# The second down projection reads its split weights and activations 64 bytes further in their partitions

## The chip, the cores and the metric
One core of one Trainium2 chip. The metric is the device time of the whole program in microseconds (us), as the median of several runs.

## What is computed
Two decoder blocks in float32, one after the other, on 512 tokens of width 1024, each with a mixing part and a feed-forward part (FFN). What matters here is the second block's FFN, whose last product is the second down projection:

```python
FFN_HIDDEN = 2816
h = rms_norm_2(x, norm_ffn_g[l])
up = causal_dwconv(h @ w_up[l], conv_ffn_w[l])
a, b = jnp.split(up, 2, axis=-1)
x = x + (jax.nn.silu(a) * b) @ w_down[l]     # [512, 2816] @ [2816, 1024]
...
return rms_norm_2(x, norm_f_g)
```

## The kernel before
**Split products.** TensorE multiplies in fp32r, so each float32 operand is kept as a high part (ScalarE's copy to fp32r) and a low part (VectorE's difference of the float32 value and the high part). Each product is three matmuls into the same place of PSUM: high by high, high by low, low by high. In most stages the weights are the stationary operand (loaded into the array, 128 columns) and the activations move (256 or 512 columns): `product` at L2516, L2519 and L2522, and lines L2783 to L2785 and L2857 to L2859. In the value projections of both blocks (`slab_v`) and in the second down projection it is the other way round: the activations are stationary and 512 columns of weights move. The profile names a matmul's operands as psum<-moving,stationary.

**Weights.** They come from memory in slabs of up to 2048 float32 values a partition, into `raw`, `x_buf`, `y_buf` and other homes. ScalarE writes a slab's high part into `w_hi` in two halves (L989, L990) and VectorE its low part into `w_lo` (L1541, L1544). `w_hi` and `w_lo` are rings of two slabs, 4096 values a partition; `W_AT[s]` is where slab s starts, and `w_at` (L660) gives the view that both the writers and TensorE use. TensorE waits for `w_lo_half` or `w_lo_ready` before a slab, and ScalarE waits for TensorE to be done with the slab that was there before.

**The second down projection.** It is computed as seven products of half the rows, half the hidden width and half the columns (`PRODUCTS`), some on sums of quarters, each in three parts (`SUBS`: 4, 4 and 3 chunks of 128 hidden values). So there are 21 weight slabs and 21 activation parts. A part of 1024 or 768 values a partition is split by ScalarE into `part_hi` (`split_part`, L1136) and by VectorE into `part_lo` (L1785), both of 11 chunks of 256 tokens. For each chunk k and each 128 tokens m of its half, `rows_product` makes three matmuls with the 128 token columns stationary and 512 weight columns moving: 21 parts, 77 chunks, 154 calls. Its lines are L3065 (high, high), L3066 (high, low) and L3067 (low, high). After parts 1 and 4 TensorE also transposes x (`turn_x`, L3054). The first down projection uses the same `part_hi` and `part_lo` as moving operands of 256 columns (L2857 to L2859). After the last product the rows are summed, normalised and stored.

**The order of the work** is written out by hand for each engine, with semaphores between them; nothing is planned at run time.

**Where operands start.** Every tensor has a fixed byte offset within a partition, from the sizes of those allocated ahead of it. Within these tensors every operand of a split product starts at a multiple of 512 bytes. Offsets before:

| tensor | byte offset | past a multiple of 128 |
|---|---|---|
| w_hi | 49280 | 0 |
| w_lo | 65664 | 0 |
| act_hi, act_lo | 104640, 121024 | 64 |
| m_hi | 137408 | 64 |
| part_hi and s_hi0 (s_at) | 182464 | 64 |
| part_lo | 193728 | 64 |
| x_buf0 | 204992 | 64 |

The moving and stationary operands of the split products outside these (s_lo, s2_hi, s2_lo, m_lo, z_hi, z_lo) also start 64 bytes past a multiple of 128.

Of the kernel before, what the change touches and what calls it, by code (L numbers as in the profile page):

```python
# [14 lines left out]
F32 = mybir.dt.float32  # L15
F32R = mybir.dt.float32r
BF16 = mybir.dt.bfloat16
ALU = mybir.AluOpType
ACT = mybir.ActivationFunctionType

P = 128
# [13 lines left out]
SLAB = 2048  # L35
COLS_A = SLAB // DC
ROWS_B = SLAB // WIDTH
FFN_STEPS = FF // COLS_A
CAUSAL = sum(TOKENS - P * b for b in range(TB))
HALF = TOKENS // 2  # L40
KH = FC // 2
# [27 lines left out]
def _add(w, kind, k0, nk, c0, nc_, home=None):  # L69
    SLABS.append((w, kind, k0, nk, c0, nc_))  # L70
    HOME.append(home or ("raw", sum(h[0] == "raw" for h in HOME), 0))
    return len(SLABS) - 1


def _cols_a(w, c0, n):
    first = len(SLABS)
    for j in range(n // COLS_A):
        _add(w, "A", 0, DC, c0 + j * COLS_A, COLS_A)
    return first
# [15 lines left out]
def _seven(w):  # L95
    first = len(SLABS)
    for place, stage, (kh, nh), _ in PRODUCTS:
        for j, (k0, nk) in enumerate(SUBS):
            _add(w, "B", kh * KH + k0, nk, nh * WIDTH, WIDTH, (place, j, stage) if place != "raw" else None)
    return first  # L100
# [5 lines left out]
S_K = _cols_a("w_in", 3 * WIDTH, WIDTH)  # L106
S_V = _add("w_in", "B", 0, ROWS_B, 4 * WIDTH, WIDTH)
_add("w_in", "B", ROWS_B, ROWS_B, 4 * WIDTH, WIDTH)
S_OUT_LRU = _add("w_out", "B", 0, WC, 0, WIDTH)
_add("w_out", "B", 0, WC, WIDTH, WIDTH)  # L110
S_OUT_ATT = _add("w_out", "B", WC, WC, 0, WIDTH)
_add("w_out", "B", WC, WC, WIDTH, WIDTH)
FIRST_SEVEN, LAST = 2, FFN_STEPS - 1

# [36 lines left out]
S_DOWN = _seven("w_ffn_out")  # L151
# [35 lines left out]

S_V2 = _add("w_in_2", "B", 0, ROWS_B, 5 * WIDTH, WIDTH)
_add("w_in_2", "B", ROWS_B, ROWS_B, 5 * WIDTH, WIDTH)
S_OA2 = _add("w_out_attn_2", "B", 0, WC, 0, WIDTH)  # L190
# [40 lines left out]
S_DOWN2 = _seven("w_down_2")  # L231
# [3 lines left out]
W_AT, W_PREV = [], []  # L235
# [76 lines left out]
def bank_of(g):  # L312

    if g == GROUP[S_F2]:
        return OUT_BANKS[0]
    if g == GROUP[S_Q2B]:
        return bank_of(GROUP[S_K2 + 1])
    return 2 if g == GROUP[S_Q2] else 4 * (g % 2)
# [56 lines left out]
def two_blocks(nc, t, out):  # L375
    with ExitStack() as ctx:
        def sb(name, shape, dt=F32, where=None):
            return (where or ctx).enter_context(nc.sbuf_tensor(name, shape, dt))

        def sem(name):  # L380
            return ctx.enter_context(nc.semaphore(name))
# [2 lines left out]
        x_base = (nc.sbuf_base + 31) // 32 * 32  # L384
        xT = sb("xT", [P, DC, TOKENS])
        raw = sb("raw", [P, 2, SLAB])
        w_hi = sb("w_hi", [P, 2, SLAB], F32R)
        w_lo = sb("w_lo", [P, 2, SLAB], F32R)
        scratch_base = (nc.sbuf_base + 31) // 32 * 32
        tmp = sb("tmp", [P, 6, TOKENS])  # L390
        rstd = sb("rstd", [P, 3, TOKENS])
# [19 lines left out]
        scope = ExitStack()  # L411
        hid = sb("hid", [P, FC, TOKENS], F32, scope)
        part_hi = sb("part_hi", [P, KH * HALF], F32R, scope)
        part_lo = sb("part_lo", [P, KH * HALF], F32R, scope)
        x_buf = [sb("x_buf0", [P, SLAB], F32, scope), sb("x_buf1", [P, SLAB], F32, scope),
                 sb("x_buf2", [P, 3 * WIDTH], F32, scope)]
        hid_at = act_base + 8 * DC * TOKENS
        s_at = hid_at + 4 * FC * TOKENS
        xg = nc.alloc_sbuf_tensor_at("xg", [P, DC, TOKENS], F32, offset=hid_at + 4 * 12 * TOKENS)
        s_hi = [nc.alloc_sbuf_tensor_at(f"s_hi{k}", [P, WC * HALF], F32R, offset=s_at + d) for k, d in enumerate((0, 8192, 28672, 36864))]  # L420
        s_lo = [nc.alloc_sbuf_tensor_at(f"s_lo{k}", [P, WC * HALF], F32R, offset=s_at + 4096 + d) for k, d in enumerate((0, 8192, 28672, 36864))]
# [132 lines left out]
        sum_made, part_hi_ready, part_lo_ready = sem("sum_made"), sem("part_hi_ready"), sem("part_lo_ready")  # L554
# [84 lines left out]
        def quarter(n):  # L639

            kh, th = PRODUCTS[n // 3][3]
            k0, nk = SUBS[n % 3]
            return hid[:, kh * KH + k0:kh * KH + k0 + nk, th * HALF:(th + 1) * HALF]
# [5 lines left out]
        def part_view(x, n):  # L649

            k0, nk = SUBS[n % 3]
            return x[:, k0 * HALF:(k0 + nk) * HALF].rearrange("p (k n) -> p k n", k=nk)
# [6 lines left out]

        def w_at(x, s, a, n):  # L660

            return x.rearrange("p a n -> p (a n)")[:, W_AT[s] + a:W_AT[s] + a + n]

        gates, gate_conv, rest_2, kept_1 = scratch[:, 2:4], scratch[:, 4:6], scratch[:, 0], scratch[:, 8]

# [308 lines left out]
        def _(act):  # L974
            A = nc.scalar.activation
# [151 lines left out]
            def split_part(n, s_down=S_DOWN):  # L1127

                if n >= N_PARTS:
                    return  # L1130
                if n >= 3:
                    act.wait_ge(slab_done, s_down + n - 2)
                made = {1: 0, 3: 3, 4: 6, 5: 9}.get(n // 3)
                if made is not None:
                    act.wait_ge(sum_made, made + n % 3 + 1 + (12 if s_down == S_DOWN2 else 0))
                A(part_view(part_hi, n), quarter(n), ACT.Copy).then_inc(part_hi_ready, 1)  # L1136

            def keep_product(bank, dst):

# [26 lines left out]
            for e in range(S_FFN + 1, S_DOWN):  # L1166
# [23 lines left out]
                if (kind, i) == ("p5", LAST - 1):  # L1190
                    act.wait_ge(slab_done, e + 1)
                    for n in range(3):
                        split_part(n)
            act.wait_ge(ffn_hidden, 2 * FFN_STEPS)
            for n in range(N_PARTS - 1):
# [222 lines left out]
            for e in range(S_UP + 2 * SECOND_SEVEN + 1, S_DOWN2):  # L1418
# [34 lines left out]
                if (kind, i) == ("p5", LAST - 1):  # L1453
                    act.wait_ge(slab_done, e + 1)
                    act.wait_ge(up_hidden, 12)
                    for n in range(3):
                        split_part(n, S_DOWN2)
# [23 lines left out]
            for n in range(N_PARTS - 1):  # L1481
                split_w(S_DOWN2 + n + 2)
                split_part(n + 3, S_DOWN2)
                if n in (2, 5):
                    act.wait_ge(up_hidden, 2 * LAST)
                    act.wait_ge(ffn_hidden, 2 * FFN_STEPS + 2)
                    act.wait_ge(slab_done, S_DOWN2 + n + 1)
# [23 lines left out]
        def _(dve):  # L1511
            V = nc.vector
# [267 lines left out]
            def split_part(n, second=0):  # L1780

                if n >= N_PARTS:
                    return
                dve.wait_ge(part_hi_ready, n + 1 + N_PARTS * second)
                V.tensor_tensor(part_view(part_lo, n), quarter(n), part_view(part_hi, n).bitcast(F32),  # L1785
                                ALU.subtract).then_inc(part_lo_ready, 1)

            def gate_out(i, b):
# [51 lines left out]
            def first_sum_lo(k):  # L1840

                dve.wait_ge(sums_hi_ready, k + 1)
                V.tensor_tensor(s_lo[k].rearrange("p (k n) -> p k n", k=WC), xg_block(*SUM_PLACE[k]),
                                s_hi[k].rearrange("p (k n) -> p k n", k=WC).bitcast(F32), ALU.subtract).then_inc(sums_lo_ready, 1)

            for e in range(S_FFN, S_DOWN):
# [49 lines left out]
                if (kind, i) == ("p4", FIRST_SEVEN):  # L1896
                    first_sum_lo(1)
            dve.wait_ge(ffn_hidden, 2 * FFN_STEPS)

# [507 lines left out]
            dve.wait_ge(up_hidden, 2 * LAST)  # L2407
            dve.wait_ge(ffn_hidden, 2 * FFN_STEPS + 2)

# [81 lines left out]
        def _(pe):  # L2491
# [22 lines left out]
            def product(dst, stationary, moving, first, last, after_one=None, after_two=None):  # L2514

                ins = mm(dst, stationary[0], moving[0], start=first, stop=False)  # L2516
                if after_one:
                    after_one(ins)
                ins = mm(dst, stationary[0], moving[1], start=False, stop=False)  # L2519
                if after_two:  # L2520
                    after_two(ins)
                return mm(dst, stationary[1], moving[0], start=False, stop=last)  # L2522

            def w_part(s, k, c0, n):

                at = k * SLABS[s][5] + c0
                return w_at(w_hi, s, at, n), w_at(w_lo, s, at, n)

            def act_part(chunk, t0=0, n=TOKENS):
                return act_hi[:, chunk, t0:t0 + n], act_lo[:, chunk, t0:t0 + n]  # L2530
# [28 lines left out]
            def slab_v(s, part, before=lambda k: None, first=range(TB), ahead=lambda tb: None):  # L2559
# [4 lines left out]
                b = bank_of(GROUP[s])  # L2564
                for k in range(ROWS_B):
                    before(k)
                    for tb in first if k == 0 else range(TB):
                        if k == 0:
                            ahead(tb)
                        ins = product(psum[:, b + tb], act_part(ROWS_B * part + k, tb * P, P), w_part(s, k, 0, WIDTH),  # L2570
                                      part == 0 and k == 0, part == 1 and k == ROWS_B - 1)
# [33 lines left out]
            for s in range(S_V):  # L2605
# [7 lines left out]
                if s == 0:  # L2613
# [3 lines left out]
                    n = NROWS - FIRST_ROWS  # L2617
# [244 lines left out]
            pe.wait_ge(z_m0, LAST - FIRST_SEVEN)  # L2862
            pe.wait_ge(ffn_hidden, 2 * FFN_STEPS - 2)
            for n in range(N_PARTS):
# [193 lines left out]
            def rows_product(n, k, m):  # L3058

                dst = psum[:, PRODUCT_BANK[n // 3] + m]  # L3060
                fresh = n % 3 == 0 and n // 3 not in (2, 4) and k == 0
                at = (SUBS[n % 3][0] + k) * HALF + m * P
                hi, lo = part_hi[:, at:at + P], part_lo[:, at:at + P]
                wh, wl = w_part(S_DOWN2 + n, k, 0, WIDTH)
                mm(dst, hi, wh, start=fresh, stop=False, skip_group_check=True)  # L3065
                mm(dst, hi, wl, start=False, stop=False, skip_group_check=True)  # L3066
                return mm(dst, lo, wh, start=False, stop=True, skip_group_check=True)  # L3067
# [79 lines left out]
```

## Time and profile before

| | us |
|---|---|
| median of 3 runs | 1256.82 |
| lowest and highest run | 1256.01, 1268.97 |
| span of the profiled execution, first to last instruction | 1253.8 |

The profile records one execution; it gives its span, and no other time of its own. The span leaves out what lies before the first and after the last instruction, so it stands beside the runs, not among them. A matmul's record is longer than the distance to the next one's start, since they are pipelined: the pace is read from starts. Offsets of tensors are not in the profile; they are in the table above.

### The profile page before, as it was taken

Reading aid. Unit: us, or ns where it says so; the run is one execution under the profiler, and the core shown is the slowest. Engines: PE = TensorE matmul, PEld = TensorE weight load, DVE = VectorE, ACT = ScalarE, POOL = GpSimd, SP = SyncE. Lnnn points to the kernel's source line nnn. Section 1 sums busy time; section 2 is a strip of 40 time slices with the busy share of each in tenths; the row PEclk is TensorE's granted clock in tenths of the full one; section 3 lists DMA queues with packets and bytes.
Section 4 is the critical chain, followed back from the end, with each engine's and each line's share of the span. In section 5 each row is a group of like instructions: output and inputs, shape, how many; then the busy total and the mean of one; then the engine's idle time right before and its main releaser. Section 6 shows DMA issues by size and latency. Waiting matters only on the chain.

```text
span 1253.8 us, 19172 instructions
## 1 busy us (share of the span) xinstructions
PE 1228.0 (98%) x7804; PEld 1078.1 (86%) x7804; DVE 991.8 (79%) x1196; ACT 670.4 (53%) x837; POOL 186.0 (15%) x168
## 2 busy tenths in 40 slices
PE   6999999999999999999999999999999999999997
PEld 5778677889999999997899999657888999988886
DVE  6888764888788778887989967566678899989886
ACT  5463674374545445567545535363444666656555
POOL 5003001002222101110122113000000222202020
PEclk9999999999999999999999999999999999999999
DMA  5423201249999779664599857301324799968765
GB/s 172 143 68 98 70 1 34 84 123 194 177 208 184 142 204 248 141 123 118 111 210 197 190 101 206 113 1 34 117 86 151 125 213 194 183 157 173 207 116 137
DMA packets 144458, 174.14 MB, mean 139 GB/s; under 512 B 5370, under 2 KB 118250, under 8 KB 144242
## 3 DMA queue, kind: packets, MB, share of 16 engines
q0 software_dynamic: 58288, 71.33, 35.7%
q1 hardware_dynamic: 86066, 101.58, 24.3%
q8 instruction: 62, 1.02, 0.3%
q14 instruction: 26, 0.21, 0.1%
q10 hardware_dynamic: 16, 0.00, 0.0%
HBM read 170.78 MB, written 2.11 MB: 138 GB/s over the span
## 4 chain that ended last, share of the span: by engine, by line
PE 92%; DVE 4%; ACT 2%; issue 1%; DMA 0%; SPq 0%; ACTq 0%; DVEq 0%
PE psum L2516 12%; PE psum L2522 12%; PE psum L2519 12%; PE psum L2785 11%; PE psum L2783 11%; PE psum L2784 11%; PE psum L2857 3%; PE psum L2859 3%; PE psum L2858 3%; PE psum L3065 2%; PE psum L3066 2%; PE psum L3067 2%; PE psum L2974 1%; PE psum L2660 1%; PE psum L2645 1%; PE psum L2672 1%
## 5 line engine op out<-in xcount | busy, mean ns | idle before, releaser
L990 ACT ACTIVATE w_hi<-raw 128x1024 fp32r<-128x1024 f32 (+2 forms) x121 | 156.2, 1294 | 210.5 <-PE psum L2522 145.6
L1544 DVE TENSOR_TENSOR w_lo<-raw,w_hi 128x1024 fp32r<-128x1024 f32 (+2 forms) x121 | 184.4, 1526 | 57.2 <-ACT w_hi L990 57.2
L2516 PE MATMUL psum<-act_hi,w_hi 128*128 128x512 f32 x520 | 207.7, 399 | 4.3 <-DVE act_lo L1551 1.5
L2522 PE MATMUL psum<-act_hi,w_lo 128*128 128x512 f32 x520 | 204.7, 394 | 0.1
L2519 PE MATMUL psum<-act_lo,w_hi 128*128 128x512 f32 x520 | 203.6, 391 | 0.0
L2785 PE MATMUL psum<-s_hi,w_lo 128*128 128x256 f32 x704 | 194.9, 277 | 0.0
L2783 PE MATMUL psum<-s_hi,w_hi 128*128 128x256 f32 x704 | 194.8, 277 | 0.0
L2784 PE MATMUL psum<-s_lo,w_hi 128*128 128x256 f32 x704 | 194.8, 277 | 0.0
L2785 PE MATMUL psum<-act_hi,w_lo 128*128 128x256 f32 x528 | 146.2, 277 | 0.0
L2783 PE MATMUL psum<-act_hi,w_hi 128*128 128x256 f32 x528 | 146.1, 277 | 0.0
L2784 PE MATMUL psum<-act_lo,w_hi 128*128 128x256 f32 x528 | 146.1, 277 | 0.0
L2784 PEld LDWEIGHTS psum<-s_lo,w_hi 128*128 128x128 f32 x704 | 132.2, 188 | 0.2
L2783 PEld LDWEIGHTS psum<-s_hi,w_hi 128*128 128x128 f32 x704 | 132.0, 188 | 0.2
L2785 PEld LDWEIGHTS psum<-s_hi,w_lo 128*128 128x128 f32 x704 | 132.2, 188 | 0.0
L2516 PEld LDWEIGHTS psum<-act_hi,w_hi 128*128 128x128 f32 x520 | 97.6, 188 | 31.0 <-issue 6.4
L2519 PEld LDWEIGHTS psum<-act_lo,w_hi 128*128 128x128 f32 x520 | 97.7, 188 | 22.6 <-issue 1.7
L2522 PEld LDWEIGHTS psum<-act_hi,w_lo 128*128 128x128 f32 x520 | 97.7, 188 | 20.8
L2784 PEld LDWEIGHTS psum<-act_lo,w_hi 128*128 128x128 f32 x528 | 99.1, 188 | 0.3
L2783 PEld LDWEIGHTS psum<-act_hi,w_hi 128*128 128x128 f32 x528 | 99.0, 188 | 0.3
L2785 PEld LDWEIGHTS psum<-act_hi,w_lo 128*128 128x128 f32 x528 | 99.1, 188 | 0.0
L1544 DVE TENSOR_TENSOR w_lo<-xz,w_hi 128x1024 fp32r<-128x1024 f32 x60 | 73.2, 1220 | 21.8 <-ACT w_hi L990 20.1
L2857 PE MATMUL psum<-part_hi,w_hi 128*128 128x256 f32 x308 | 85.0, 276 | 0.0
(411 smaller groups left out, 2672.6 us busy)
## 6 DMA issues: line engine op xcount, KB each, us to landing
raw<-in_w_in SPq DMA_DIRECT2D x15, 1024.0 KB, 5.4
xz<-in_w_ffn_in POOLq DMA_DIRECT2D x24, 512.0 KB, 6.6
raw<-in_w_ffn_in SPq DMA_DIRECT2D x22, 512.0 KB, 5.5
xz<-in_w_up POOLq DMA_DIRECT2D x21, 512.0 KB, 6.1
raw<-in_w_up SPq DMA_DIRECT2D x18, 512.0 KB, 5.2
raw<-in_w_in SPq DMA_DIRECT2D x16, 512.0 KB, 5.0
v<-in_w_in POOLq DMA_DIRECT2D x15, 512.0 KB, 6.2
x_buf<-in_w_ffn_out POOLq DMA_DIRECT2D x6, 1024.0 KB, 9.8
```

The lines of the kernel that those rows point to most:

```text
L990: A(w_at(w_hi, s, h, n - h), home(s, n)[:, h:n], ACT.Copy).then_inc(w_hi_ready, 1)
L1544: V.tensor_tensor(w_at(w_lo, s, h, n - h), home(s, n)[:, h:n], w_at(w_hi, s, h, n - h).bitcast(F32), ALU.subtract).then_inc(w_lo_ready, 1)
L2516: ins = mm(dst, stationary[0], moving[0], start=first, stop=False)
L2519: ins = mm(dst, stationary[0], moving[1], start=False, stop=False)
L2522: return mm(dst, stationary[1], moving[0], start=False, stop=last)
L2783: mm(dst, wh, hi, start=kind not in ("p2", "p4") and k == 0 and m == 0, stop=False, skip_group_check=True)
L2784: mm(dst, wh, lo, start=False, stop=False, skip_group_check=True)
L2785: ins = mm(dst, wl, hi, start=False, stop=True, skip_group_check=True)
L2857: mm(dst, wh, hi, start=fresh, stop=False, skip_group_check=True)
L2858: mm(dst, wh, lo, start=False, stop=False, skip_group_check=True)
L2859: return mm(dst, wl, hi, start=False, stop=True, skip_group_check=True)
L3065: mm(dst, hi, wh, start=fresh, stop=False, skip_group_check=True)
```

## The change
The second down projection uses operands that lie 64 bytes further. The two weight buffers become flat and 32 values longer, so that slabs from `S_DOWN2` on can start 16 values (64 bytes) later in them; the activation parts of the second down projection get views `row_hi` and `row_lo` that start 64 bytes past `part_hi` and `part_lo`; a pad of 32 values stands behind `part_lo`. ScalarE and VectorE write, and TensorE reads, through the moved views. With the longer buffers, `w_lo` starts 128 bytes later, all tensors behind it 256 bytes later, and `x_buf` 384. In the second down projection the moving operands then start at 49344 (w_hi) and 65856 (w_lo), 64 bytes past a multiple of 128, and the stationary ones at 182784 and 194048, on a multiple. Everything else keeps its offset within 128 bytes.

```diff
+MOVED = 16
...
-        w_hi = sb("w_hi", [P, 2, SLAB], F32R)
-        w_lo = sb("w_lo", [P, 2, SLAB], F32R)
+        w_hi = sb("w_hi", [P, 2 * SLAB + 2 * MOVED], F32R)
+        w_lo = sb("w_lo", [P, 2 * SLAB + 2 * MOVED], F32R)
...
         part_lo = sb("part_lo", [P, KH * HALF], F32R, scope)
+        sb("part_rest", [P, 2 * MOVED], F32, scope)
...
+        row_hi = nc.alloc_sbuf_tensor_at("row_hi", [P, KH * HALF], F32R, offset=s_at + 4 * MOVED)
+        row_lo = nc.alloc_sbuf_tensor_at("row_lo", [P, KH * HALF], F32R, offset=s_at + 4 * KH * HALF + 4 * MOVED)
...
         def w_at(x, s, a, n):
 
-            return x.rearrange("p a n -> p (a n)")[:, W_AT[s] + a:W_AT[s] + a + n]
+            at = W_AT[s] + (MOVED if s >= S_DOWN2 else 0)
+            return x[:, at + a:at + a + n]
...
-                A(part_view(part_hi, n), quarter(n), ACT.Copy).then_inc(part_hi_ready, 1)
+                A(part_view(part_hi if s_down == S_DOWN else row_hi, n), quarter(n), ACT.Copy).then_inc(part_hi_ready, 1)
...
-                V.tensor_tensor(part_view(part_lo, n), quarter(n), part_view(part_hi, n).bitcast(F32),
+                hi, lo = (row_hi, row_lo) if second else (part_hi, part_lo)
+                V.tensor_tensor(part_view(lo, n), quarter(n), part_view(hi, n).bitcast(F32),
                                 ALU.subtract).then_inc(part_lo_ready, 1)
...
-                hi, lo = part_hi[:, at:at + P], part_lo[:, at:at + P]
+                hi, lo = row_hi[:, at:at + P], row_lo[:, at:at + P]
```

## Rows read from the trace of the kernel before
**Rows 1.** the page of the kernel before: head, busy table, granted clock
```profile
span 1253.8 us, 19172 instructions
...
PE 1228.0 (98%) x7804; PEld 1078.1 (86%) x7804; DVE 991.8 (79%) x1196; ACT 670.4 (53%) x837; POOL 186.0 (15%) x168
...
PEclk9999999999999999999999999999999999999999
```
**Rows 2.** the page: the chain that ended last, by engine
```profile
PE 92%; DVE 4%; ACT 2%; issue 1%; DMA 0%; SPq 0%; ACTq 0%; DVEq 0%
```
**Rows 3.** one line's instructions: L3065 between 1165.5 and 1246 us
```profile
L3065 PE MATMUL psum<-w_hi,part_hi x116: 393/398/479, 1165.3 to 1245.8; 128*128 128x512 f32 x116
```
**Rows 4.** the same view: L2516 between 922.4 and 976.5 us
```profile
L2516 PE MATMUL psum<-act_hi,w_hi x79: 388/388/397, 922.7 to 976.2; 128*128 128x512 f32 x79
```
**Rows 5.** stretches: window, length, TensorE busy (instructions seen), granted clock, DMA share, GB/s
```profile
632.00:672.00 40.00, 40.00 (x342) 1.00 1.03 208
934.00:974.00 40.00, 40.00 (x177) 1.00 0.37 120
1000.00:1040.00 40.00, 40.00 (x355) 1.00 0.99 192
```
**Rows 6.** timeline of TensorE at 778 us; start us, us, engine, line, out<-moving,stationary
```profile
778.43 0.40 PE L2516 MATMUL psum<-w_hi,act_hi 128*128 128x512 f32 x1
...
779.13 0.39 PE L2516 MATMUL psum<-w_hi,act_hi 128*128 128x512 f32 x1
...
779.83 0.40 PE L2516 MATMUL psum<-w_hi,act_hi 128*128 128x512 f32 x1
```
**Rows 7.** timeline of TensorE across the start of the second down projection
```profile
1134.69 0.28 PE L2784 MATMUL psum<-act_lo,w_hi 128*128 128x256 f32 x1
1134.80 0.28 PE L2785 MATMUL psum<-act_hi,w_lo 128*128 128x256 f32 x1
1134.92 0.39 PE L3065 MATMUL psum<-w_hi,part_hi 128*128 128x512 f32 x1
...
1135.61 0.39 PE L3065 MATMUL psum<-w_hi,part_hi 128*128 128x512 f32 x1
...
1137.01 0.39 PE L3065 MATMUL psum<-w_hi,part_hi 128*128 128x512 f32 x1
```
**Rows 8.** timeline of TensorE across 618 us
```profile
616.96 0.39 PE L2516 MATMUL psum<-act_hi,w_hi 128*128 128x512 f32 x1
...
618.33 0.28 PE L2783 MATMUL psum<-act_hi,w_hi 128*128 128x256 f32 x1
...
619.04 0.28 PE L2783 MATMUL psum<-act_hi,w_hi 128*128 128x256 f32 x1
```
**Rows 9.** one line's instructions: L2516 between 54.5 and 64.8 us
```profile
L2516 PE MATMUL psum<-act_hi,w_hi x15: 397/397/398, 54.7 to 64.5; 128*128 128x512 f32 x15
```
**Rows 10.** waits between 1130 and 1254 us: total us, times, longest
```profile
ACT w_hi L989 <- PE psum L3067: 31.4, 16, 3.1
...
PEld psum L3065 <- DVE w_lo L1541: 0.5, 1, 0.5
```
**Rows 11.** stretch 1182 to 1222 us: PE, PEld, DVE, ACT, POOL busy, clock, DMA
```profile
1182.00:1222.00 40.00, 40.00 (x173) 32.25 (x172) 36.80 (x35) 22.90 (x29) 7.80 (x6) 1.00 0.51 89
```
**Rows 12.** groups of ScalarE by shape, 1134 to 1254 us
```profile
L1136 ACT ACTIVATE part_hi<-hid 128x1024 fp32r<-128x1024 f32 x12 | 12.6, 1047 | 5.9 <-DVE hid L1911 5.9
L989 ACT ACTIVATE w_hi<-x_buf 128x1024 fp32r<-128x1024 f32 x7 | 7.4, 1056 | 6.4 <-PE psum L3067 6.0 <-PE psum L2785 0.5
```
**Rows 13.** groups of TensorE by shape, whole span
```profile
L2516 PE MATMUL psum<-act_hi,w_hi 128*128 128x512 f32 x520 | 207.7, 399 | 4.3 <-DVE act_lo L1551 1.5 <-DVE act_lo L1553 1.5 <-DVE w_lo L1544 0.6
...
L2783 PE MATMUL psum<-s_hi,w_hi 128*128 128x256 f32 x704 | 194.8, 277 | 0.0
...
L2783 PE MATMUL psum<-act_hi,w_hi 128*128 128x256 f32 x528 | 146.1, 277 | 0.0
...
L2857 PE MATMUL psum<-part_hi,w_hi 128*128 128x256 f32 x308 | 85.0, 276 | 0.0
```

## The prediction
> **What bounds the kernel now.** I read the head of the page first. TensorE is busy 98% of a span of 1253.8 us, and its granted clock is 9 tenths or more in every slice, so the clock stays at the higher of its two levels (2.4 GHz) and takes no part in what follows [rows 1]. Then the chain that ended last: 92% of it is TensorE, so the time is the number of matmuls times the distance between their starts, and little else [rows 2]. A busy share of 98% says nothing of that distance, because a matmul's record overlaps the next one's. So I took starts.
>
> In the second down projection 116 starts of L3065 lie between 1165.3 and 1245.8 us. Each is followed by one of L3066 and one of L3067, so 115 x 3 = 345 steps take 80.5 us: 233.3 ns a step [rows 3]. In the first slabs of the second FFN, also 512 columns wide, 79 starts of L2516 lie between 922.7 and 976.2 us: 78 x 3 = 234 steps in 53.5 us, 228.6 ns a step [rows 4]. Both stretches run without a stop and at the same clock. The stage that the change touches is thus paced about 4.7 ns a matmul slower than its neighbour.
>
> Two more places tell what goes with the slow pace. The value projection of the second block is built as the down projection is, with split weights moving and split activations stationary; six steps from 778.43 to 779.83 us are 1.40 us, again 233.3 ns [rows 6]. And the pace changes at the border, with no stop between: up to 1134.80 us the steps of 256 columns are 0.11 us, and from 1135.61 to 1137.01 us six steps of the down projection take 1.40 us [rows 7]. What the two slow stages share is where their operands start. By the offsets in the section on the kernel, moving w_hi and w_lo start on a multiple of 128 bytes and stationary activations 64 bytes past one. In every other split product of the kernel it is the other way round.
>
> The slow pace is not bound to those offsets alone. At 618.33 us the steps go from 228 ns (616.96 to 618.33 us is 1.37 us for six) at 512 columns to 118 ns (0.71 us for six) at 256 [rows 8], and they stay there: of 40 us the stretch at 632 us holds 342 matmuls and the one at 1000 us 355 [rows 5]. 40/342 less 40/355 is 4.3 ns, the same surplus per matmul, though those activations move from 64 bytes past a multiple of 128. So do those of 54.7 to 64.5 us, where 42 steps take 9.8 us, 233.3 ns [rows 9]. I read this as two paces between which TensorE's stream falls: moving operands on a multiple of 128 always got the long one (the value projections and all of the down projection), the others nearly always the short one.
>
> **The change, part by part.** It adds no instruction, no wait and no DMA.
>
> *Buffers.* w_hi and w_lo grow by 128 bytes a partition each, and a pad of 128 bytes stands ahead of the x buffers. So w_lo starts 128 bytes later, everything allocated behind it 256, and x_buf 384. All of these are multiples of 128, so no product outside the second down projection changes its offset within 128 bytes. DMA, ScalarE and VectorE do the same work at addresses of the same kind: cost 0.
>
> *Moved writers.* For the 21 weight slabs ScalarE and VectorE write 64 bytes further, and for the 21 activation parts too. Rows of both kinds of address exist: copies of 128x1024 to part_hi (64 past) take 1047 ns, and to w_hi (on the multiple) 1056 ns [rows 12]. They swap, so the sum over the stage is bounded by 9 ns each way for each of some 60 copies, 0.5 us of ScalarE's time. None of it is on the path: ScalarE waits 31.4 us in this stage for TensorE to give buffers back, against 0.5 us that TensorE waits for VectorE's w_lo [rows 10]. I take 0.
>
> *Moved operands of TensorE.* 154 x 3 = 462 matmuls. Afterwards the moving weights start 64 bytes past a multiple of 128 and the stationary activations on one, which is the arrangement of rows 4. If the pace goes with it, each step shrinks by 4.7 ns by rows 3 and 4, or 4.3 ns by the pair in rows 5: 462 x 4.7 = 2.2 us or 462 x 4.3 = 2.0 us. I take 2.1 us. The bounds are 0 (the pace doesn't care) and, below nothing, nothing that a row shows for this stage: it already has the longest pace that any split product of its width has.
>
> The Trainium skill has a rule that would make the gain larger. In "TensorE: Matmul & The Clock Gate", section "Back-to-back issue gap", a warm matmul of N columns costs N/2.4 + 2.5 ns, which is 215.8 ns for 512. An estimate by that page is (233.3 - 215.8) x 462 = 8.1 us. No long stretch of this trace goes below 228.6 ns [rows 4], so the measurement decides and the sum stays at 2.1 us.
>
> *The feeders.* If TensorE wants its slabs 2% sooner, ScalarE and VectorE must give them sooner. Between 1182 and 1222 us TensorE is busy all 40 us, VectorE 36.8, ScalarE 22.9 [rows 11]. The 173 matmuls seen there would need about 0.8 us less; VectorE has 3.2 us to spare. Its cover thins but holds, and were it gone, the stage would keep at most its old pace. Nothing new is late after the last matmul: mean square, root, scaling and store follow as before.
>
> *Sum.* 1253.8 - 2.1 = 1251.7 us of span. The profile gives no time of its own beside the span; the median of the runs shown, 1256.82 us, lies 3.0 us above it. With the same 3.0 us the forecast is 1254.7 us, 0.17% faster, where about 1% is what a measurement of this kernel tells from no change.
>
> **The rivals.**
>
> *The offset does nothing: 1256.8 us.* The down projection is slow for another reason, say that its weights come through the moving side, or that its stream starts in the long pace after the two rounds of transposes at L3054 and stays there. For it: the long pace also occurs with the good offsets [rows 8, 9], so offset and pace are not one thing. Against it: form and operand sizes are those of rows 4, and the switch at the border of the stage comes with no pause [rows 7].
> The Trainium skill speaks for this rival too: "SBUF — State Buffer", section "Who interferes with whom", gives TensorE two independent read ports, one for the moving operand and one for the weight load, that never wait for anyone, and its note on cachelines makes 16 bytes the unit; by both a shift of 64 bytes changes nothing. That the trace has two paces at one clock doesn't fit these rules by itself.
>
> *The change also frees the stretch of 618 to 714 us: 1251.2 us.* All buffers behind w_hi move, so that stream may fall into the short pace. Some 96 us / 0.1177 us = 816 steps by 4.3 ns are 3.5 us more, 1254.7 - 3.5. For it: nothing in offsets within 128 bytes holds that stretch in the long pace, so something finer does. Against it: the same something may be the timing of its first step, which isn't touched.
>
> *A long stretch outside falls into the long pace: slower.* The distance from w_hi to w_lo goes from 16384 to 16512 bytes in every stage, and the split products load from both in turn. If that distance, or the address within 256 bytes (of which w_lo's changes), selects the pace, stretches that are short now become long. Outside the touched stage there are at least (520 + 704 + 528 + 308) x 3 = 6180 such matmuls [rows 13], less the 816 and 48 that are long already: about 5300 at 4.3 ns is 22.8 us, and the time is 1254.7 + 22.8 = 1277.5 us, 1.6% slower. It decides from about 490 matmuls on (2.1 us / 4.3 ns), where the gain is eaten, and from 3400 on it is over 1%. For it: rows 8 show that one border suffices to turn over 800 matmuls. Against it: of the long streams with moving operands 64 past, only two short or middling ones turned.
>
> **How the numbers follow.** Offset selects the pace: 0.68, 1254.7 us. No effect: 0.19, 1256.8 us. Also the stretch at 618 us: 0.07, 1251.2 us. A stretch outside turns long: 0.06. The range runs from 1250.5 us (the third case, less the 0.8 us by which the two nearest runs of the kernel before differ) to 1260.0 us: no effect, 0.8 us of spread, and a stretch of some 550 matmuls turned long (2.4 us). The whole of the last rival is left out. Faster by over 1% needs 12.6 us, which no case gives: 0.02. Slower by over 1% needs more than half of all matmuls outside to turn, or something unseen: 0.04. Within 1%: 0.94.
>
> **What would show it.** Right: the line view of L3065 has a step of about 229 ns instead of 233.3 in its last 80 us, the durations of its records fall from a median of 398 ns towards 390, a window of 40 us there holds some 176 matmuls instead of 173, and from the first matmul of the stage to its last it is about 2 us shorter. The value projection at 778 us stays at 233.3 ns. The copies to w_hi in that stage take about 1050 ns. Wrong: the step of L3065 stays at 233.3 ns (second case); the counts of 40 us at 632 or 1000 us change (the other two); or TensorE waits more than 1 us for w_lo in this stage, which would mean that VectorE's cover is gone.

## The result, and the profile after

| | us |
|---|---|
| changed kernel, median of 6 runs (lowest, highest) | 1272.07 (1271.17, 1273.75) |
| kernel before, median of 6 runs (lowest, highest) | 1256.45 (1254.03, 1268.97) |
| ratio, with its 95% interval | 1.0111 (1.0083 to 1.0139) |
| span of the profiled execution, before and after | 1253.8, 1271.1 |

The kernel got 1.1% slower, where 0.2% faster was forecast. The page of the changed kernel, as far as it answers to [rows 1, 2]: head, busy table, granted clock and the chain that ended last, by engine.

```profile
span 1271.1 us, 19172 instructions
...
PE 1245.7 (98%) x7804; PEld 1093.2 (86%) x7804; DVE 994.7 (78%) x1196; ACT 671.5 (53%) x837; POOL 186.3 (15%) x168
...
PEclk9999999999999999999999999999999999999999
...
PE 95%; ACT 2%; DVE 2%; DMA 0%; issue 0%; SPq 0%; ACTq 0%
```

The same number of instructions, the same clock, and 17.7 us more of TensorE. The chain is TensorE still. So the steps got longer, and the first thing to see is where. One line's instructions (durations, first and last start): L2863 is the first matmul of the *first* down projection, which has 256 columns and no operand moved. First the kernel before, then the changed one.

```profile
L2857 PE MATMUL psum<-part_hi,w_hi x308: 276/276/276, 460.6 to 564.9; 128*128 128x256 f32 x154
```

```profile
L2863 PE MATMUL psum<-part_hi,w_hi x308: 278/279/280, 469.8 to 579.3; 128*128 128x256 f32 x154
```

From the first to the last of these 308 starts, 307 x 3 = 921 steps take 104.3 us before and 109.5 after: 113.2 and 118.9 ns a step. So a stage that the diff only displaces pays 5.2 us, more than the whole forecast. TensorE over stretches of 40 us, first the kernel before and then the changed one; the number in brackets counts matmuls:

```profile
320.00:360.00 40.00, 40.00 (x355) 1.00 0.97 198
665.00:705.00 40.00, 40.00 (x342) 1.00 0.96 181
```

```profile
320.00:360.00 40.00, 40.00 (x339) 1.00 0.93 184
665.00:705.00 40.00, 40.00 (x339) 1.00 1.00 192
1010.00:1050.00 40.00, 40.00 (x356) 1.00 1.02 200
```

At 320 us 355 matmuls became 339. At 665 us the kernel before was already slow (342), and it got a little slower (339). Of these three stretches only the one at 1010 us runs as before [rows 5]. In the second down projection itself, first the kernel before, then the changed one:

```profile
L3065 PE MATMUL psum<-w_hi,part_hi x154: 393/396/504, 1134.9 to 1245.8; 128*128 128x512 f32 x154
```

```profile
L3071 PE MATMUL psum<-w_hi,row_hi x154: 388/394/483, 1153.4 to 1263.1; 128*128 128x512 f32 x154
```

The stage takes 110.9 us from its first to its last start before, and 109.7 after: 1.2 us less, where 2.1 were forecast. The border of the stage, in the timeline (start, duration), answers to [rows 7]:

```profile
1153.25 0.28 PE L2791 MATMUL psum<-act_hi,w_lo 128*128 128x256 f32 x1
1153.37 0.39 PE L3071 MATMUL psum<-w_hi,row_hi 128*128 128x512 f32 x1
...
1154.06 0.40 PE L3071 MATMUL psum<-w_hi,row_hi 128*128 128x512 f32 x1
...
1155.45 0.39 PE L3071 MATMUL psum<-w_hi,row_hi 128*128 128x512 f32 x1
```

Six steps from 1154.06 to 1155.45 us take 1.39 us, 231.7 ns against 233.3 before. Over the whole stage the mean of triples of steps is 231.2 ns. The feeders answer to [rows 10], and nothing is wrong with them:

```profile
ACT w_hi L994 <- PE psum L3073: 30.8, 16, 3.0
...
PEld psum L3071 <- DVE w_lo L1546: 0.2, 1, 0.2
```

**Where the 17.3 us of span come from.** All steps of split products from the two traces' starts, taken three by three, with pauses left out:

| products | matmuls | ns a step before | after | us |
|---|---|---|---|---|
| 256 columns, activations move | 4620 | 114.12 | 117.57 | +15.9 |
| 512 columns, activations move | 1848 | 229.24 | 231.41 | +4.0 |
| value projections, weights move | 192 | 233.33 | 231.32 | -0.4 |
| second down projection, weights move | 462 | 233.32 | 231.19 | -1.0 |

The sum is 18.5 us. The 1.2 us by which the spans differ less lie in stops and at the borders of streams, which this count leaves out. The line to note is the third. The value projections got 2 ns a step shorter as well, though none of their operands was moved by 64 bytes.

### The profile page after: what moved, and what is told of

The parts are those of the page before. It is cut to its first block, busy times and chain, and to the rows that moved or that the text cites. A ratio compares the mean times of both kernels' runs of the same rounds, so it can differ in the third digit from the quotient of the medians.

```text
span 1271.1 us, 19172 instructions
## 1 busy us (share of the span) xinstructions
PE 1245.7 (98%) x7804; PEld 1093.2 (86%) x7804; DVE 994.7 (78%) x1196; ACT 671.5 (53%) x837; POOL 186.3 (15%) x168
## 3 DMA queue, kind: packets, MB, share of 16 engines
q8 instruction: 62, 1.02, 0.3%
## 4 chain that ended last, share of the span: by engine, by line
PE 95%; ACT 2%; DVE 2%; DMA 0%; issue 0%; SPq 0%; ACTq 0%
PE psum L2522 12%; PE psum L2528 12%; PE psum L2525 12%; PE psum L2790 12%; PE psum L2789 11%; PE psum L2791 11%; PE psum L2864 3%; PE psum L2863 3%; PE psum L2865 3%; PE psum L3073 3%; PE psum L3071 3%; PE psum L3072 3%; PE psum L2980 1%; PE psum L2666 1%; PE psum L2651 1%; PE psum L2678 1%
## 5 line engine op out<-in xcount | busy, mean ns | idle before, releaser
L2522 PE MATMUL psum<-act_hi,w_hi 128*128 128x512 f32 x520 | 210.5, 405 | 4.3 <-DVE act_lo L1558 1.7
L2790 PE MATMUL psum<-s_lo,w_hi 128*128 128x256 f32 x704 | 197.8, 281 | 0.0
L2864 PE MATMUL psum<-part_lo,w_hi 128*128 128x256 f32 x308 | 87.2, 283 | 0.0
```

The source lines that it names most:

```text
L2790: mm(dst, wh, lo, start=False, stop=False, skip_group_check=True)
L2864: mm(dst, wh, lo, start=False, stop=False, skip_group_check=True)
```

## The experiments

All time differences of under 0.5% or so drown in the spread of the kernel before (31 runs of one comparison lie between 1254.7 and 1270.1 us), so the step is the reading that decides and the time its check. "Distance" below is the byte offset of the moving operand less that of the stationary one, within 256. Before it is 64 for w_hi and w_lo alike where activations move, and 192 where weights move. In the changed kernel w_lo lies 128 bytes later and the activations 256, so the distance of w_lo is 192 in the first case and 64 in the second, while that of w_hi stays.

### Is it the 64 bytes, or the longer buffers?

**grow_only.** The buffers of the changed kernel, without the moves.
```diff
-            at = W_AT[s] + (MOVED if s >= S_DOWN2 else 0)
+            at = W_AT[s]
...
-offset=s_at + 4 * MOVED)
+offset=s_at)
...
-offset=s_at + 4 * KH * HALF + 4 * MOVED)
+offset=s_at + 4 * KH * HALF)
```


> The changed kernel with its buffers as long as there (w_lo 128 bytes later, all behind it 256), but with no operand moved by 64 bytes: the second down projection reads where the buffers begin. Theory A, the pace of a split product follows the distance between its moving and its stationary operand (bytes, within 256), so that w_lo's 128 bytes cost the time and the 64 bytes, which both operands share, do nothing: about 1272 us, as the changed kernel, and steps of 231.1 ns in the second down projection, as there. Theory B, the 64 bytes cost or give something: the time leaves 1272 us by more than 3 us, or the step of L3065 goes back to 233.3 ns. Theory C, all of it is luck of how streams start: anything between 1254 and 1272 us.

Measured: 1272.7 us, ratio to before 1.0101 (1.0073 to 1.0129). The stage of the second down projection and two stretches of 40 us:

```profile
L3071 PE MATMUL psum<-w_hi,row_hi x154: 387/394/478, 1152.8 to 1262.5; 128*128 128x512 f32 x154
```

```profile
320.00:360.00 40.00, 40.00 (x339) 1.00 0.94 184
1010.00:1050.00 40.00, 40.00 (x355) 1.00 1.02 200
```

109.7 us for the stage and 339 matmuls at 320 us: the readings of the changed kernel, without its 64 bytes. Both its loss and its small gain come from the longer buffers.

**wide256.** The changed kernel, moves and all, with w_hi and w_lo longer by 256 bytes instead of 128.
```diff
-        w_hi = sb("w_hi", [P, 2 * SLAB + 2 * MOVED], F32R)
-        w_lo = sb("w_lo", [P, 2 * SLAB + 2 * MOVED], F32R)
+        w_hi = sb("w_hi", [P, 2 * SLAB + 4 * MOVED], F32R)
+        w_lo = sb("w_lo", [P, 2 * SLAB + 4 * MOVED], F32R)
```


> The changed kernel with w_hi and w_lo longer by 256 bytes instead of 128, the 64-byte moves kept. w_lo then lies 256 bytes later than before and everything behind it 512. Theory A (distance within 256 bytes): every distance is that of the kernel before, so about 1256 us, with the second down projection at 233.3 ns a step in spite of its moved operands. Theory B (the 64 bytes matter): the second down projection isn't at 233.3 ns. If the distance counts within 512 bytes or more, the time stays near 1272 us.

Measured: 1256.68 us, ratio 0.9978 (0.9944 to 1.0013).

```profile
L3071 PE MATMUL psum<-w_hi,row_hi x154: 389/397/499, 1134.9 to 1245.8; 128*128 128x512 f32 x154
```

```profile
320.00:360.00 40.00, 40.00 (x356) 1.00 0.96 196
1010.00:1050.00 40.00, 40.00 (x355) 1.00 0.99 193
```

The loss is gone (356 matmuls at 320 us), and so is the gain: 110.9 us for the stage, 233.3 ns a step, with the moving operands 64 bytes past a multiple of 128 and the stationary ones on it. That is the arrangement on which the forecast rested, and it does nothing.

**all64.** The kernel before with 64 unused bytes ahead of w_hi.
```diff
+        sb("pad", [P, 16])
         w_hi = sb("w_hi", [P, 2, SLAB], F32R)
```


> The kernel before with 64 unused bytes ahead of w_hi, so that all tensors from w_hi on lie 64 bytes later and every distance between them stays. Theory A (distances): no change, 1254 to 1258 us, 233.3 ns in the down projection. The theory of the prediction (where the moving operand starts within 128 bytes): weights move 64 past a multiple of 128 and get 229 ns, and all other moving operands start on a multiple and get the long step, 5300 matmuls by 4.3 ns, about 1277 us.

Measured: 1260.89 us (1257.38 to 1271.33), ratio 1.0011 (0.9975 to 1.0047). 111.0 us for the stage, 355 matmuls at 320 us.

```profile
L3066 PE MATMUL psum<-w_hi,part_hi x154: 389/395/496, 1140.0 to 1251.0; 128*128 128x512 f32 x154
```

```profile
320.00:360.00 40.00, 40.00 (x355) 1.00 0.97 196
1010.00:1050.00 40.00, 40.00 (x346) 1.00 1.00 197
```

Every operand of the split products changed its offset within 128 bytes. The steps stayed: 229.3 ns where 512 columns of activations move, 233.3 where weights do, and at 256 columns the two paces that the kernel before has too (113.3 and 117.8 ns). By the forecast's reading this kernel was to take 1277 us. The stretch at 1010 us holds both of them (346 matmuls); more of that below.

**lo_only128.** The kernel before with w_lo and the scratch behind it 128 bytes later, and everything from act_hi on in its place.
```diff
         w_hi = sb("w_hi", [P, 2, SLAB], F32R)
+        decay = sb("decay", [P, WC])
+        f_bias = sb("f_bias", [HEADS, 1])
+        eps = sb("eps", [P, 2])
+        gain_both = sb("gain_both", [P, DC])
         w_lo = sb("w_lo", [P, 2, SLAB], F32R)
...
-        decay = sb("decay", [P, WC])
-        f_bias = sb("f_bias", [HEADS, 1])
-        eps = sb("eps", [P, 2])
-        gain_both = sb("gain_both", [P, DC])
```


> The kernel before with w_lo and the scratch tensors behind it 128 bytes later and nothing else: four small tensors of 128 bytes together go from behind the scratch to between w_hi and w_lo, so act_hi, part_hi and all later tensors stay. Theory A (distance of moving and stationary operand within 256 bytes): the distances are those of the changed kernel, 64 from w_hi and 192 from w_lo where activations move, so about 1272 us and 118.9 ns in most 256-column streams. If it was the shift of the activations by 256 bytes instead: 1254 to 1270 us, as before.

Measured: 1280.38 us, ratio 1.0172 (1.0121 to 1.0223).

```profile
L3065 PE MATMUL psum<-w_hi,part_hi x154: 388/394/478, 1161.8 to 1271.5; 128*128 128x512 f32 x154
```

```profile
320.00:360.00 40.00, 40.00 (x339) 1.00 0.94 184
1010.00:1050.00 40.00, 40.00 (x339) 1.00 0.96 191
```

The stage takes 109.7 us and the stretch at 320 us has 339 matmuls, as in the changed kernel, so the place of w_lo is enough (of the scratch that moved with it nothing is an operand of a split product). The time is 8 us above the expected. At 1010 us there are 339 matmuls here and 356 in the changed kernel: that stream of 1104 matmuls runs at 118.9 ns instead of 113.3, 6.1 us, and the products of 512 columns at 232.6 ns instead of 231.4, another 2.2 us.

### Does the distance set the pace?

**rows128.** The kernel before, only the activations of the second down projection 128 bytes further.
```diff
+        sb("part_rest", [P, 32], F32, scope)
...
+        row_hi = nc.alloc_sbuf_tensor_at("row_hi", [P, KH * HALF], F32R, offset=s_at + 4 * 32)
+        row_lo = nc.alloc_sbuf_tensor_at("row_lo", [P, KH * HALF], F32R, offset=s_at + 4 * KH * HALF + 4 * 32)
```
(and the uses of the two views as in the change.)

> The kernel before, and only the split activations of the second down projection 128 bytes further (w_hi and w_lo as before, a pad of 128 bytes ahead of x_buf). Moving less stationary address goes from 192 to 64 within 256 bytes, what the products with moving activations had before. Theory A: the step of L3065 falls from 233.3 to about 229 ns, 462 x 4.3 ns = 2.0 us less, the rest as before: about 1254 us. The theory of the prediction (offsets within 128 bytes): 233.3 ns, no change.

Measured: 1258.14 us, ratio 0.9967 (0.9929 to 1.0004), which is no difference that can be told.

```profile
L3069 PE MATMUL psum<-w_hi,row_hi x154: 388/394/501, 1137.1 to 1246.6; 128*128 128x512 f32 x154
```

109.5 us for the stage with 228.9 ns a step, where the kernel before has 110.9 and 233.3. The offsets within 128 bytes are those of before, so only the distance is new (x_buf moved too, but no product reads it). This is the gain that the forecast looked for; 462 x 4.4 = 2.0 us of it should show, and 1.4 do. In this execution TensorE's weight loads waited 0.8 us for w_lo in the stage and stood still another 0.4 us for no reason that the profile shows, against 0.5 us in all before.

**rows192** is the same with 192 bytes (`4 * 48`), so that the distance is 0.

> The kernel before, and only the split activations of the second down projection 192 bytes further, so that its moving and stationary operands are 0 apart within 256 bytes, the distance at which act192 had the shortest step for 512 columns (226.8 ns in this stage). Theory A: 226.8 ns a step against 233.3 ns, 462 x 6.5 = 3.0 us less than the kernel before in that stage, the streams elsewhere as before and with their luck: a median of 1252 to 1258 us. If the gain in act192 came from the whole kernel being shifted: 233.3 ns.

Measured: 1256.75 us, ratio 0.9995 (0.9965 to 1.0024).

```profile
L3069 PE MATMUL psum<-w_hi,row_hi x154: 387/389/504, 1135.4 to 1244.2; 128*128 128x512 f32 x154
```

```profile
PEld psum L3069 <- DVE w_lo L1544: 0.9, 1, 0.9
PEld psum L3069 <- issue: 0.5, 1, 0.5
```

The stage takes 108.8 us, 2.1 us less than before, at 226.8 ns a step. Two stops that the kernel before has only in part (0.9 and 0.5 us) eat the rest of the 3.0 us. The whole kernel can't be told from the one before: a stage's 2 us are below what the runs resolve.

**act32, act64, act128, act192, act224**: the kernel before with so many unused bytes behind w_lo, here for 64.
```diff
         w_lo = sb("w_lo", [P, 2, SLAB], F32R)
+        sb("pad", [P, 16])
```


> The kernel before with 64 unused bytes behind w_lo: weights stay, everything behind them lies 64 bytes later, so the distance of moving and stationary operand within 256 bytes goes from 64 to 128 where activations move, and from 192 to 128 where weights move. Theory A (distance sets the pace): both kinds of product get the same pace, one that the kernel before doesn't show; if pace grows with the distance it lies between 229 and 233.3 ns at 512 columns. If only offsets of one operand mattered, weights that move would stay at 233.3 ns.

> The kernel before with 128 unused bytes behind w_lo. Activations that move are then 192 from the weights, which is what the down projection had before, and weights that move are 64 from the activations. Theory A: the paces change sides: about 229 ns in the second down projection and the value projections (2.9 us less), 233.3 ns and about 118 ns always where activations move (some 5500 matmuls by 4.3 ns or more, 24 us and up): about 1277 to 1284 us. Theory of the prediction (offset within 128 bytes): nothing changes, 1254 to 1260 us.

> The kernel before with 192 unused bytes behind w_lo: all distances are 0 within 256 bytes. Theory A: one pace for both kinds of product. By a reading in which the two streams of reads meet in the same place it is the longest of all; by one in which they then run in step it is the shortest. Either way far from the time before if pace and distance are tied: below 1250 or above 1262 us.

> The kernel before with 32 unused bytes behind w_lo: distance 96 where activations move, 160 where weights move. Theory A with a pace that grows smoothly with the distance: between before (64) and act64 (128) for moving activations. If only whole steps of 64 bytes count, it equals one of the two.

> The kernel before with 224 unused bytes behind w_lo: distance 32 where activations move, 224 where weights move. Fills the gap between 0 (act192) and 64 (before). Theory A: paces between these two, so 227 to 229 ns at 512 columns; at 256 columns 113.3 to 120 ns. If steps of 64 bytes count alone, it equals act192 or the kernel before. Any value that all 256-column streams keep below 117 ns would be a place without luck.

Measured, as ratios to before: act32 1289.06 us, 1.0245 (1.02 to 1.0291); act64 1283.74 us, 1.0205 (1.0167 to 1.0242); act128 1270.25 us (1259.55 to 1272.22), 1.0071 (1.0038 to 1.0103); act192 1275.7 us, 1.0141 (1.0104 to 1.0178); act224 1274.25 us, 1.0126 (1.0082 to 1.0169). For act128, the stage and the two stretches of 40 us; then the stage and the same stretches for act192:

```profile
L3066 PE MATMUL psum<-w_hi,part_hi x154: 388/394/505, 1150.0 to 1259.2; 128*128 128x512 f32 x154
```

```profile
320.00:360.00 40.00, 40.00 (x342) 1.00 0.94 186
1010.00:1050.00 40.00, 40.00 (x355) 1.00 1.03 205
```

```profile
L3066 PE MATMUL psum<-w_hi,part_hi x154: 389/389/499, 1157.7 to 1266.1; 128*128 128x512 f32 x154
```

```profile
320.00:360.00 40.00, 40.00 (x336) 1.00 0.91 182
1010.00:1050.00 40.00, 40.00 (x335) 1.00 1.00 196
```

With act128 the sides are changed: the stage runs at 228.9 ns, and all 512-column products with moving activations at 233.3. With act192 the stage is the shortest of all (108.4 us), while 256 columns are at their slowest (336). Stretches of act32, of act64 and of act224:

```profile
320.00:360.00 40.00, 40.00 (x336) 1.00 0.91 182
1010.00:1050.00 40.00, 40.00 (x335) 1.00 0.96 183
```

```profile
320.00:360.00 40.00, 40.00 (x336) 1.00 0.92 182
1010.00:1050.00 40.00, 40.00 (x339) 1.00 0.97 188
```

```profile
320.00:360.00 40.00, 40.00 (x345) 1.00 0.96 188
1010.00:1050.00 40.00, 40.00 (x345) 1.00 1.02 199
```

All kernels together: the steady paces, from the starts in their traces, in ns a step (activations moving, or weights moving where marked *). The mean of a stage or of a kind of product lies up to 0.6 ns above them, since it holds borders and short stretches of another pace.

| distance | 512 columns | 256 columns |
|---|---|---|
| 0 (act192; rows192*) | 226.7; 226.7* | 120.0 |
| 32 (act224) | 233.3 | 116.7 or 117.8 |
| 64 (before; rows128*) | 228.9, one stretch 233.3; 228.9* | 113.3 or 117.8 |
| 96 (act32) | 233.3 | 120.0 |
| 128 (act64) | 232.6; 232.5* | 118.7 or 120.0 |
| 160 (act32) | 234.2* | |
| 192 (act128; before*) | 233.3; 233.3* | 113.3 or 117.8 |
| 224 (act224) | 233.3* | |
| w_hi 64, w_lo 192 (changed kernel) | 228.9 or 233.3 | 118.9, one stream 113.3 |
| w_hi 192, w_lo 64 (changed kernel) | 231.2* | |

At each distance where both kinds were seen (0, 64, 128 and 192, all at 512 columns), it doesn't matter which of the operands moves. The distance decides which paces occur, with no simple order: for 512 columns 0 is best and 64 next; for 256 columns 0 is worst and only 64 and 192 reach 113.3. In the last two rows w_hi and w_lo lie at different distances, and there the distance of each matmul by itself doesn't give the pace: 118.9 ns is longer than both paces seen at 64 alone and at 192 alone (113.3 and 117.8). Whether the change from one distance to the other counts, or the distance between w_hi and w_lo, no run separates.

My expectations of act128 (256 columns always long), act32 (between its neighbours) and act224 (512 columns near 228 ns) were wrong, because the paces don't follow the distance in order.

### Two paces at one distance

Three more profiles of unchanged kernels, the kernel before twice and the changed one once.

> The kernel before, unchanged, profiled once more. If the pace of a 256-column stream is drawn anew in each execution, the streams at 289, 458, 618, 750 and 980 us (113.3 but for 618 us, which had 117.8) come out otherwise here, and the span with them: 4.45 ns for each of their 1248, 948, 816, 240 and 1104 matmuls that turns. If addresses and program alone decide, they come out as in the first profile and the span is 1253.8 us within 1 us.

> The kernel before, unchanged, a third profile: as for the second. The runs of this kernel so far lie between 1254 and 1270 us; with 4.45 ns a matmul the streams that turn should account for the difference of this span from 1253.8 us within 1 us.

> The changed kernel, unchanged, profiled once more. Theory A with two paces: the first four 256-column streams at 118.9 ns again, and a time of 1270 to 1274 us; the fifth, of 1104 matmuls, which had 113.3 ns in its first profile, may come out at 118.9 ns and the span 6.1 us longer. If the fifth is short by its place in the program, it is at 113.3 ns again.

Measured: 1255.98 us (span 1254.2), 1257.5 us (span 1255.7), and 1275.01 us (span 1273.3) for the changed one. TensorE in the stream at 618 us, first before_again, then before_third:

```profile
640.00:655.00 15.00, 15.00 (x134) 1.00 1.14 215
665.00:705.00 40.00, 40.00 (x355) 1.00 0.96 182
```

```profile
640.00:655.00 15.00, 15.00 (x135) 1.00 1.08 213
665.00:705.00 40.00, 40.00 (x342) 1.00 0.96 182
```

In the first profile of this same program the stretch from 665 us held 342 matmuls. Here it holds 355 and 342, and at 640 us the third profile still has the short pace (135 in 15 us). Between them, at 658 us, TensorE stopped for 1.6 us, and the stream came back in the long one. So the pace isn't set by program and addresses alone, nor by the chip: before_again and before_third ran on the same one. A stream takes one of its paces where it starts, and keeps it for hundreds of matmuls until something breaks its rhythm. A stop can turn it or leave it (before_again stopped for 0.3 us at 659 us and came back at 113.3 ns), and it takes no stop: in all64 a single step of 134 ns at 1022 us, 20 ns longer than the others, is where the stream goes from 113.3 to 117.8 ns for good:

```profile
1022.11 0.28 PE L2786 MATMUL psum<-s_hi,w_lo 128*128 128x256 f32 x1
1022.23 0.30 PE L2784 MATMUL psum<-s_hi,w_hi 128*128 128x256 f32 x1
1022.36 0.28 PE L2785 MATMUL psum<-s_lo,w_hi 128*128 128x256 f32 x1
```

The stream at 750 us came out at 113.3 ns in the first and at 117.8 in the other two. Each distance has its own set of paces. In after_again the four long streams at 290, 467, 633 and 766 us ran at 118.9 ns again; the fifth began at 113.3 again, changed to 118.9 behind one step of 161 ns at 1076 us, and has a mean of 115.7, stops included. Two of its stretches of 30 us:

```profile
1045.00:1075.00 30.00, 30.00 (x267) 1.00 0.98 188
1090.00:1120.00 30.00, 30.00 (x255) 1.00 0.84 163
```

My expectation that the turned streams account for the span within 1 us failed. In before_again the stream at 618 us has the short pace for 816 matmuls, 3.6 us less, and yet the span is 0.4 us longer. The waits of before_again between 600 and 760 us say why:

```profile
PEld psum L2516 <- DVE w_lo L1544: 2.6, 1, 2.6
PEld psum L2783 <- issue: 0.2, 1, 0.2
```

TensorE got to the end of the stream sooner and then waited 2.6 us for w_lo. With that, 1.1 us of the turned stream at 750 us, 0.5 us of short streams between 719 and 744 us that turned too, and the stop of 0.3 us, the account comes to 0.9 us more, against 0.4 measured. No such wait is in the first profile. Behind this stream the supply of weights took back most of what the short pace gave. In before_third as many matmuls turned short (360 of the stream at 618 us) as turned long (360 between 720 and 778 us), and the span is 1.9 us longer: there the stops count, 1.6 us at 658 us and 1.1 us for w_lo at the end of that stream.

## Why the prediction was wrong

**The step that failed is "Buffers": "All of these are multiples of 128, so no product outside the second down projection changes its offset within 128 bytes [...] cost 0."** The premise holds and the conclusion doesn't: the products outside cost about 20 us (the first two lines of the table of steps), because w_lo's 128 bytes change where it lies, within 256 bytes, against the activations and against w_hi. grow_only (1272.7 us) shows the whole cost without any moved operand, wide256 (1256.7 us) its absence with all of them, and lo_only128 (1280.4 us) that w_lo's place is enough for it.

**"Moved operands": 462 x 4.3 to 4.7 ns = 2.1 us.** The stage gave 1.2 us, for another reason, so it was luck that it went the forecast way at all. Its two operands move by the same 64 bytes, so their distance stays; wide256 has them and keeps 233.3 ns. The 2 ns a step came from w_lo's 128 bytes, as the value projections show, which got them too. The evidence I used [rows 3, 4, 6, 7] couldn't separate two readings. Where weights move, the offset within 128 bytes and the distance within 256 are both the reverse of the usual, in all places. I took the offset and had no row that spoke for it over the distance.

**The rivals.** "A long stretch outside falls into the long pace" is what happened. Its price of 22.8 us was close to the 19.9 us of the first two lines of the table of steps, and I gave it 0.06. It named the distance from w_hi to w_lo, or the address within 256 bytes. The runs show a third thing at work, the distance between moving and stationary operand: rows128 and rows192 change the pace with both weight buffers in their places, and all64 moves both operands of every split product by 64 bytes and keeps the paces. Whether the distance from w_hi to w_lo counts beside it is open. A stretch with the good offsets at the long pace [rows 8, 9] stood in the text and said that the offset alone didn't select it, so 0.68 for the offset was more than the rows bore.

"The offset does nothing" was right on the 64 bytes. The rules that stood by it, from the Trainium skill, "SBUF — State Buffer", section "Who interferes with whom", gave the right answer for the 64 bytes and can't be carried further: from independent ports for the moving operand and the weight load I would conclude that their distance doesn't matter, and here it is worth up to 7.5 ns of a step at 512 columns (226.7 to 234.2). The stretch at 618 us, which one rival saw freed, came free in before_again with no change at all, and most of its gain was lost in a wait.

**The range.** Its lower end, 1251.2 less 0.8 us, is 1250.4 and not 1250.5 us. It left out the whole of the rival that came true, so 1272.07 us lies 12 us above its upper end.

**What held.** The bound (TensorE's steps, at one clock), the feeders (ScalarE waits 30.8 us for TensorE after, TensorE 0.2 us for w_lo), the moved writers (ScalarE's copies of 128x1024 from x_buf to w_hi take 1055 ns after, 1056 before), and that nothing much is added behind the last matmul (from the end of its record to the end of the span 7.2 us, 7.1 before).

**What stays open.** Why the distance counts isn't shown. That it counts within 256 bytes rests on wide256, and on grow_only and lo_only128, where w_lo lies 128 bytes further from the activations in one and 128 nearer in the other, with a mean step of 231.2 ns in the stage in both. What selects a pace at a stream's start wasn't tried, nor was an execution of the kernel before near 1270 us profiled, so that its long runs are streams with the long pace is argued from their size (4.45 ns for each of up to 3300 matmuls), not shown.

## What to carry to other kernels

Adding a few bytes to a buffer moves everything behind it, and in a kernel that TensorE bounds this can cost more than the edit is about: here 128 bytes were 1.1% of the time. Before a change is judged, hold the distance between moving and stationary operands (within 256 bytes) as it was, by padding in whole 256 bytes as wide256 did, and read the step from starts in stages that the change doesn't touch. Where two readings fit the same rows, look for the row in which they differ, and if there is none, don't put two thirds of the chance on one.

## What the runs showed of the hardware that I had not expected

- The step of a split matmul depends on the distance between its moving and its stationary operand in the partition, within 256 bytes, at an unchanged clock (1.00 in every stretch shown): 226.7 to 234.2 ns for 512 columns, 113.3 to 120.0 ns for 256, and what is best for the one (0) is worst for the other.
- At one distance there can be two steady paces. A stream keeps one for hundreds of matmuls, a stop or a single step 20 ns too long can turn it, and the same program can have another in another execution (342 or 355 matmuls in the same 40 us).
- The Trainium skill, "TensorE: Matmul & The Clock Gate", section "Back-to-back issue gap", gives N/2.4 + 2.5 ns, 215.8 ns for 512 columns, as the gap of an isolated matmul, and about 131 ns for one in a stream of weight loads and matmuls. The shortest steady step in any of the runs is 226.7 ns (act192 and rows192), longer than both, so the measurement decides.
